# Reordering the output products, the VectorE copies and the output additions in the compressed and selected attention loop of a two-block transformer kernel

## What is computed

```
o_cmp = softmax(q k_cmp + bias) v_cmp                 # 31 compressed keys
o_slc = softmax(q ks + bias, causal) vs               # selected blocks
o_win = softmax(q kw + bias, causal, last 512) vw     # window
o = g0 * o_cmp + g1 * o_slc + g2 * o_win              # gates per head and token
y = sigmoid(g_conv) * conv_out + sigmoid(g_attn) * o
```

## Time and profile before

| | |
|---|---|
| median of three executions | 2017.85 us (2015.47 to 2018.05) |
| profiled execution, time | 2011.72 us |
| profiled execution, span of its instructions | 2009.9 us |
| busy over the span: TensorE, VectorE, ScalarE, GpSimd | 94%, 38%, 30%, 31% |
| the loop of 64 units | from 1278 to 1437 us of the span, 8% of it |
| TensorE clock granted in that stretch | 1.00 |

### The profile page before, as it was taken

How to read it: one execution, slowest core, us unless ns; L and a number is a source line. 1 busy time by engine, 2 the same in 40 slices (tenths; PEclk the granted TensorE clock), 3 DMA queues, 4 the chain that set the end, 5 groups by cost and what they waited for, 6 DMA issues and landing times.

```text
span 2009.9 us, 22143 instructions
## 1 busy us (share of the span) xinstructions
PE 1893.5 (94%) x8716; PEld 1220.1 (61%) x8716; DVE 762.4 (38%) x1551; ACT 612.0 (30%) x1111; POOL 628.7 (31%) x374
## 2 busy tenths in 40 slices
PE   5999999999989989989999999899899999999998
PEld 3554337634333333368887868544577678888786
DVE  6552266523222222262899225366340220000002
ACT  3112562311011011062223344466343342232212
POOL 0000432011011010054443325555434235555532
PEclk9999999999999999999999999999999999999999
DMA  9452003889999999963224321110142023322321
GB/s 383 168 211 87 32 22 131 316 359 426 428 427 427 428 428 428 396 217 111 84 84 126 105 84 67 49 33 22 64 157 84 1 95 101 109 84 88 122 84 63
DMA packets 90037, 358.29 MB, mean 178 GB/s; under 512 B 6955, under 2 KB 35883, under 8 KB 75484
## 3 DMA queue, kind: packets, MB, share of 16 engines
q1 hardware_dynamic: 87088, 351.75, 45.1%
q0 software_dynamic: 2304, 4.20, 0.6%
q10 hardware_dynamic: 556, 1.13, 0.1%
HBM read 355.42 MB, written 5.83 MB: 180 GB/s over the span
## 4 chain that ended last, share of the span: by engine, by line
PE 75%; DMA 13%; DVE 5%; ACT 3%; issue 2%; POOL 1%; SPq 0%; POOLq 0%; DVEq 0%; ACTq 0%
PE bank L754 14%; PE bank L756 14%; PE bank L755 14%; PE bank L729 11%; DMA slots<-in_w_expert_gate 9%; PE bank L1160 7%; DMA slots<-in_w_expert_up 3%; PE bank L1373 2%; PE bank L1393 2%; PE bank L881 1%; PE bank L1362 1%; PE bank L1131 1%; PE bank L1185 1%; ACT area L1983 1%; DMA slots<-in_w_ada 1%
## 5 line engine op out<-in xcount | busy, mean ns | idle before, releaser
L2815 POOL TENSOR_TENSOR low_r<-slots,high_r 128x2048 fp32r<-128x2048 f32 x82 | 380.0, 4634 | 511.1 <-ACT high_r L1612 511.1
L755 PE MATMUL bank<-xl_r,high_r 128*128 128x512 f32 (+1 forms) x832 | 320.3, 385 | 0.0
L754 PE MATMUL bank<-area_r,high_r 128*128 128x512 f32 x800 | 312.7, 391 | 0.0
L756 PE MATMUL bank<-area_r,low_r 128*128 128x512 f32 x800 | 311.3, 389 | 0.0
L1612 ACT ACTIVATE high_r<-slots 128x2048 fp32r<-128x2048 f32 x82 | 156.9, 1914 | 402.9 <-PE bank L756 402.1
L1160 PE MATMUL bank<-slots,area 128*64 128x512 f32 x992 | 226.8, 601 | 22.5 <-DMA slots<-in_w_expert_gate 16.2
L755 PEld LDWEIGHTS bank<-xl_r,high_r 128*128 128x128 f32 x832 | 156.3, 188 | 31.6 <-issue 0.5
L756 PEld LDWEIGHTS bank<-area_r,low_r 128*128 128x128 f32 x800 | 150.2, 188 | 31.5
L754 PEld LDWEIGHTS bank<-area_r,high_r 128*128 128x128 f32 x800 | 150.2, 188 | 31.4 <-issue 0.6
L1160 PEld LDWEIGHTS bank<-slots,area 128*64 128x64 f32 x992 | 67.5, 137 | 165.4 <-issue 126.0
L2616 DVE SCALAR_TENSOR_TENSOR bank<-area,cols,bank 128x512 f32<-128x512 f32 x232 | 153.4, 747 | 0.0
(11 more groups left out here) (423 smaller groups left out, 2811.7 us busy)
## 6 DMA issues: line engine op xcount, KB each, us to landing
slots<-in_w_expert_down SPq DMA_DIRECT2D x32, 2048.0 KB, 16.3
slots<-in_w_expert_up SPq DMA_DIRECT2D x32, 2048.0 KB, 16.2
slots<-in_w_expert_gate SPq DMA_DIRECT2D x30, 2048.0 KB, 15.0
slots<-in_w_in SPq DMA_DIRECT2D x15, 2048.0 KB, 7.9
slots<-in_w_ada SPq DMA_DIRECT2D x11, 2048.0 KB, 12.0
slots<-in_ffn_in_w SPq DMA_DIRECT2D x22, 1024.0 KB, 6.7
slots<-in_ffn_out_w SPq DMA_DIRECT2D x5, 2048.0 KB, 7.8
slots<-in_w_out SPq DMA_DIRECT2D x4, 2048.0 KB, 8.1
```

Source lines behind the costliest of these rows:

```text
L754: nc.tensor.matmul(out, xh, yh, start=start and n == 0, stop=False)
L755: nc.tensor.matmul(out, xh, yl, start=False, stop=False)
L756: last = nc.tensor.matmul(out, xl, yh, start=False, stop=stop and n == len(pairs) - 1)
L2815: nc.gpsimd.tensor_tensor(low_half(m), raw_half(m), high_half(m), ALU.subtract).then_inc(s["w_low"], 1)
```

## The change

It alters the order of instructions in four loops and no instruction itself. TensorE does O ahead of S and T in its step, where it stood behind them. VectorE does K1 of unit u - 3 in step u, where it was u - 2, ahead of A; A comes two steps later (u % 8 is 6 instead of 4). ScalarE's rounding and GpSimd's remainder of the same tile also come two steps later. The last units' leftovers behind the loops follow from that.

```diff
@@ -1408,12 +1408,12 @@
             for u in range(4 * NH):
+                if u >= 6 and u % 4 == 2:
+                    nsa_outputs(u // 4 - 1)
                 if u + 2 < 4 * NH:
                     nsa_scores(u + 2)
                 if u:
                     nsa_transposes(u - 1)
-                if u >= 6 and u % 4 == 2:
-                    nsa_outputs(u // 4 - 1)
             nsa_transposes(4 * NH - 1)
             nsa_outputs(NH - 1)
@@ -1984,10 +1984,11 @@
                 if u >= 2:
                     nsa_keep_t(u - 2)
-                if u >= 8 and u % 8 == 6:
-                    split_mixed(u // 8 - 1)
+                if u >= 16 and u % 8 == 0:
+                    split_mixed(u // 8 - 2)
             nsa_keep_t(4 * NH - 2)
             nsa_keep_t(4 * NH - 1)
+            split_mixed(NH // 2 - 2)
             split_mixed(NH // 2 - 1)
@@ -2713,13 +2714,13 @@
                 if u >= 1:
                     nsa_inverse(u - 1)
-                if u >= 8 and u % 8 == 4:
+                if u >= 3:
+                    nsa_keep_t(u - 3)
+                if u >= 14 and u % 8 == 6:
                     nsa_keep_outputs(u // 8 - 1)
-                if u >= 2:
-                    nsa_keep_t(u - 2)
             nsa_inverse(4 * NH - 1)
-            nsa_keep_t(4 * NH - 2)
-            nsa_keep_t(4 * NH - 1)
+            for u in range(4 * NH - 3, 4 * NH):
+                nsa_keep_t(u)
             nsa_keep_outputs(NH // 2 - 1)
@@ -2899,8 +2900,9 @@
-                if u >= 8 and u % 8 == 7:
-                    low_mixed(u // 8 - 1)
+                if u >= 17 and u % 8 == 1:
+                    low_mixed(u // 8 - 2)
+            low_mixed(NH // 2 - 2)
             low_mixed(NH // 2 - 1)
```

## The result

The kernel after has a median of 1999.23 us over four executions (1997.67 to 2000.92), the kernel before 2016.66 us in the same session (2014.86 to 2018.05). The ratio is **0.9917, with a 95% interval of 0.9902 to 0.9933**: 17 us faster. A second session gave 0.9913 (0.9898 to 0.9929); one of its five executions took 2755 us at a mean granted clock of 0.66 and is left out. The forecast was 2001.4 us with a range of 1996.0 to 2009.5.

What follows compares the result with a forecast made beforehand. TensorE was taken to set the pace, idle 18.4 of 159.0 us. Half-blocks (12.9 to 15.8 us) plus both ends gave 14.0 to 17.7; 16.5 was taken, hence 2001.4 us, range 1996.0 to 2009.5.

Steps and rivals of the forecast that it cites:

- the half-blocks: The 14 stretches of TensorE's loop from T0 to T0: 1.13 us saved in each, 15.8 us in all.
- the lower bound: Gain in the loop's 14 half-blocks counted by the rows' idle time alone: 0.92 us each, 12.9 us.
- the start: Start of the loop, where K1 of unit 0 kept VectorE waiting with R(3) behind: 0 to 0.8 us gained, 0.6 taken.
- the end: End of the loop: the 1.42 us wait before T of unit 61 goes, some 0.3 us comes back: 1.1 us gained.
- The dense half-block: One half-block without C in which TensorE never waits: 7.96 us against 9.09 before.
- rival 2: After the loop: TensorE's idle time goes, but what follows waits for something that stays put: no change, 2017.9 us; chance 0.06.
- both gaps: TensorE's idle times between T0 and T1: 0.30 us before S0 and 0.62 us before T1, both to go.
- The slower rival: In the half-blocks, O in front holds back S0 and its chain to the next T0: slower, 2026 us; chance 0.05.
- the block of R(2) by K1(3): On VectorE, R(2) queues behind K1(3), which cannot start before 1348.45; R(2) starts at 1349.05, delaying S0 and T1.
- The room of 0.3 us: On TensorE before T0 touches bank 7: K1(3) ends at 2.67, wanted at 3.06, the least room claimed.
- the walk: One new half-block timed across the engines from the start of S2, with TensorE dense: nothing waits, next S2 at 7.96 us.
- The second look at A: A's second pass meeting GpSimd at SBUF in the loop: if each time, 4.8 us less gain, 11.7 instead of 16.5.

Runs made afterwards that it cites:

- the first experiment: The kernel before with only TensorE's O moved ahead of S and T, other engines in their old order: loop 152.27 us, ratio 0.9943 to the kernel before.

## Why the prediction was right, and where it was not

**The sum.** The loop was to become 16.5 us shorter, and did so by 16.48. The terms: the half-blocks 14.54 us (14 x 1.04) against 15.8, or 12.9 at the lower bound; the start 0.87 against 0.6; the end 1.07 against 1.1. The hit to 0.02 us is luck: my terms 15.8, 0.6 and 1.1 add up to 17.5, and I took 16.5 as a value between the bounds, with no term for the missing 1.0. The term that was too large is the half-blocks'. The dense half-block was estimated at 7.96 us and is 8.05, mostly because T0 takes 0.37 where I had put 0.30 from the eight transposes of T3. The rows had the better value: six transposes (T2) in 0.80 us and eight (T3) in 1.02 are 0.11 for each and 0.14 on top, which gives 0.36 for two. The start's 0.87 lies just above its bound of 0.8. TensorE's idle time was forecast under 4 us and is 3.2 from the first S to the end of the last O.

**The clock and the rest of the span** did what was assumed: the clock is 1.00 in the loop in both, and what follows the loop came forward with it (from the first product with `w_out` to the end of the span it takes 571.0 us before and 571.2 after), so rival 2 is out.

**O ahead** was described rightly: both gaps closed, by O's 2.3 us. The slower rival did not come: the chain S, R, E, V, M fits.

**K1 a unit later** is the step that was read wrongly. The prediction made the block of R(2) by K1(3) the mechanism, and the later copy a part of the cure. The block is real in the kernel before. But once O stands ahead, K1 can stay where it was without costing anything in the half-blocks (119.70 us both ways), and alone it makes the loop longer. The room of 0.3 us that I gave it in the walk was 0.25, so that figure was sound. In the walk R(2) starts at 0.6 and K1(3) at 1.98; measured it is 0.95 and 1.99, since K1(3) waits for T3 in any case.

**A two steps later** was undervalued. The prediction gave its old place a wait that would vanish, and no price. Its place was worth 7.9 us of the 16.5, since A's 1.4 us at the old place hold K1 back (and, with K1 at u - 2, R(1) too) where TensorE has no O to cover them. I had priced the cover of the new place (T2 waiting up to 1.4 us without O) and not the price of the old one, and my expectation for the experiment was still under half of it. Added one after the other, the parts give 8.3 us for O ahead (160.59 to 152.27), 6.7 for the place of A, rounding and remainder (to 145.58) and 1.5 for K1 later (to 144.11). Some 1.9 of the 6.7 (an estimate, 6 x 0.32 from the T0 of the first experiment) is the remainder's, which the prediction moved at no gain. Taken in another order they give other numbers: K1 later alone is worth -3.4 us. A moved alone, with O and K1 at their old places, was not run.

**The second look at A.** The rows of the kernel before had no meeting of A's second pass and M, and the prediction took none. In the kernel after there is none either, by 0.05 us (M(1) ends at 1344.80, the pass starts at 1344.85). In the other orders there are meetings: at the old place with O ahead GpSimd's pass went from 0.77 to 1.20 us, ahead of K1 M(1) went from 1.09 to 1.59, and with K1 at u - 2 it was A's pass that went from 0.69 to 0.91. A meeting did not always reach TensorE: in that last run it cost nothing. The Trainium skill (page "SBUF — State Buffer", section "Who interferes with whom") says that a VectorE instruction with two SBUF inputs and a GpSimd instruction that reads SBUF shut each other out; these traces agree in that each such meeting made one or both longer, and so does the run in which one input came from PSUM.

## What to carry to other kernels

Where an engine sets the pace in order, look for its longest piece of work whose inputs are long ready, and put it where the inputs of the next pieces are late; here that one move, 2.3 us of output products between T0 and T1, closed both gaps. Then look at each long item on the helper engines (A, 1.4 us, and the remainder, 1.3 us) and put it in the step that this cover protects: together that was worth 7 to 8 us, as much as the 8 of the first move. Try each part of such a change alone as well as all but that part: alone, the later copy looked harmful, and without it nothing was lost but 1.5 us at the ends. And look at the granted clock of each stretch before a loss is put down to waits: 4.9 us of one kernel's loop were the clock's.

## What the runs showed of the hardware

A VectorE addition with both inputs in SBUF (128x512) and a GpSimd multiplication of the same size stretched each other when they overlapped, from 0.69 to 0.78 us and from 0.77 to 1.20 us. With one of VectorE's inputs in PSUM they overlapped at 0.69 and 0.77 us. Where the addition started while a GpSimd multiplication of 128x256 was under way, it was the addition that grew, to 0.91 us. In the kernel with all but O ahead, TensorE's granted clock averaged 0.67 to 0.68 in three stretches of some 5 us that each followed a wait of about 1.6 us, and stayed at 1.00 after four other such waits. In the loop's own time the traces repeat to 0.01 us, while the start of the loop moved by up to 8 us between profiles: a change of 1.5 us is seen in the trace and not in the medians.
